# Block products of the triangular inverse in four 32-row array tiles instead of two 64-row tiles

## The chip, the cores and the metric

The kernel runs on one core of a Trainium2 chip. The metric is the device time of one execution in microseconds (us). Before the change the median of three runs is 4128.65 us (4125.22 to 4132.72). TensorE is the matmul engine, VectorE (DVE), ScalarE (ACT) and GpSimd (POOL) the others; SyncE (SP) issues some of the DMAs.

## The reference

Two blocks of two layers each, batch 1, 512 tokens, width 1024, all in float32. The first block is a hybrid of retention and HGRN2 with a gated MLP; the second has sliding-window attention, an RWKV-7 recurrence, a gated MLP and an embedding layer. Only the recurrence of the second block matters here:

```
def rwkv7_scan(r, w, k, v, a, b):           # 16 heads of 64 channels, 512 tokens
    def step(state, inp):
        r_t, w_t, k_t, v_t, a_t, b_t = inp
        sa = jnp.einsum('bhvk,bhk->bhv', state, a_t)
        state = (state * w_t[:, :, None, :] + sa[..., None] * b_t[:, :, None, :]
                 + v_t[..., None] * k_t[:, :, None, :])
        return state, jnp.einsum('bhvk,bhk->bhv', state, r_t)
    ...
```

## The kernel before

The stage is the function `rwkv_b`, run once in each of the two layers of the second block. It works on 8 pairs of heads (`PAIRS`). The 128 partitions hold two heads of 64 channels; the 512 columns are 8 chunks (`NC`) of 64 tokens (`C`). Inside a chunk the recurrence is a triangular system: with A the strictly lower 64x64 matrix of the decayed products of a and b, the kernel needs the inverse of (I - A) for each head and each chunk. The chunks themselves then follow each other in a chain.

The inverse is built by doubling. It starts from 1x1 and 2x2 diagonal blocks and runs over five levels, `INV_LEVELS = (2, 4, 8, 16, 32)`. At the level with number n, two neighbouring diagonal blocks of size n become one of size 2n. Three block products make a level, each a call of `products`:

- `lower` (the order's rows with bank 3): the matrix `mabt` (a buffer of `gate`) by the inverse so far, `xx` (a buffer of `rw_z`). ScalarE copies bank 3 to `pp` (also in `gate`) at L2116, a helper's line for nearly all of its operations in this stage.
- `inverse` (bank 5): the inverse so far by `pp`. VectorE merges the result into `xx` with a mask, by a predicated copy at L2378.
- `inverse_t` (bank 4): the transposed result, merged into `xt` (`rw_xt`) at the same line.

The last level has no `inverse`, since only the transposed form is used afterwards. A call of `products` issues one 64x64 matmul for each chunk and each head, 16 in all; a head's matmul uses the rows and columns of its own half of the array, so the two heads sit in two array tiles. Only the last matmul of a call signals. The mask takes from the result only the blocks that the level joins.

TensorE's order is written out by hand: in pair p, between every two products, `chain_on` issues one of the 24 steps of the chunk chain of pair p-1 (L1933 to L1949, also 64x64 matmuls). After each step VectorE makes a small copy (L2276, L2278, L2281) that the next step waits for. Pair 0 has no such steps between its products. The head of a pair (`dense`) holds the projections (L228 to L230, 128x512) of the pair's inputs, with weights that are streamed from HBM through a ring by GpSimd's queue.

All engines' instruction streams are unrolled over layers and pairs, so each matmul is an instruction of its own in the program.

Of the kernel before, what the change touches and what calls it, by code (L numbers as in the profile page):

```python
# [1438 lines left out]
C = 64  # L1439
NC = S // C  # L1440
# [367 lines left out]
def rwkv_b(run, io, l, ws, again, nxt, y_all, y_hi, y_lo, gate):  # L1808

    with ExitStack() as ctx:  # L1810
        sc = Stage(run, ctx, f"rw{l}")
        half = run.eps[:, 3:4]
        banks, par = run.banks, run.par_b[:, l, :]
# [3 lines left out]
        v, mabt, pp = ks, lw, cum  # L1817
        e0, e1, kn, yq = run.w[:, 0, :], run.w[:, 1, :], run.w[:, 2, :], run.acc
        z = sc.sb("z", [P, 2, S + 1])
        xx = [z[:, i, 1:S + 1] for i in range(2)]  # L1820
# [6 lines left out]
        at_, rt, mak, mrb, mrk, xt, bt, ktt, vt = ([e[:, :], o[:, :]] for e, o in zip(even, odd))  # L1827
# [17 lines left out]
        cx_made, cx_kept, xcx_made, xcxt_made = (sc.sem("cx_made"), sc.sem("cx_kept"), sc.sem("xcx_made"),  # L1845
                                                 sc.sem("xcxt_made"))
# [6 lines left out]
        LEVELS_ = len(INV_LEVELS)  # L1853
# [16 lines left out]
        def read(name, p):  # L1870

            i = place[name, p]
            who = order[i][3]
            return who, sum(e[3] is who for e in order[:i + 1])
# [6 lines left out]
        def cut(c):  # L1881
            return slice(c * C, (c + 1) * C)
# [25 lines left out]
        def _(pe):  # L1908
            def claim(name, p):

                i = place[name, p]
                for e in reversed(order[:i]):
                    if e[2] == order[i][2]:
                        pe.wait_ge(*read(*e[:2]))
                        break
                return bank(name, p)[:, :]

            def whole(name, p, lhs, rhs_, signal):
                pe.matmul(claim(name, p), lhs, rhs_, start=True, stop=True).then_inc(signal, 1)  # L1919
# [32 lines left out]
            def products(out, lhs, rhs_, signal):  # L1952

                for c in range(NC):
                    for s_ in heads:
                        mm = pe.matmul(banks[out][s_, cut(c)], lhs[s_, cut(c)], rhs_[s_, cut(c)], start=True, stop=True)  # L1956
                mm.then_inc(signal, 1)

            def dense(p):
                def decays():  # L1960
                    if p == 0:
                        pe.wait_ge(wa_made, 1)
                    pe.wait_ge(low_in[p % 2], 32 * (p // 2 + 1))
                    if p:
                        pe.wait_ge(f_free, 3 * p)
                        pe.wait_ge(x_made, 5 * p)
                    whole("w", p, lr[0:64, p % 2, :], wa[0:64, :], lr_made)
                    whole("a", p, lr[64:128, p % 2, :], wa[64:128, :], lr_made)

                if p:  # L1970
                    decays()
                if p >= 2:
                    pe.wait_ge(ysq_made, p - 1)
                    pe.wait_ge(xt_made, 6 * p)
                    whole("var", p - 2, bones[:, :], yq[:, :], var_made)
                ws.project(pe, claim("k", p), hh, hl)
                if p == 0:
                    decays()
                ws.project(pe, claim("r", p), hh, hl)
                pe.wait_ge(sq_made, p + 1)  # L1980
                if p:
                    pe.wait_ge(cx_kept, 5 * p)
                whole("ssq", p, bones[:, :], e0, ssq_made)
                ws.project(pe, claim("v", p), hh, hl)
                if p == 0:
                    pe.wait_ge(gd_made, 2)
                out = claim("g", p)
                pe.matmul(out, g2[:, p % 2, 0, :], gd[:, 0, :], start=True, stop=False)
                pe.matmul(out, g2[:, p % 2, 1, :], gd[:, 1, :], start=False, stop=True).then_inc(g_made, 1)
                pe.wait_ge(rk_made, p + 1)  # L1990
                whole("bonus", p, bones[:, :], kp, bon_made)
# [33 lines left out]
            def lower(p, i):  # L2025
                n = LEVELS_ * p + i
                pe.wait_ge(x_made, n + 1)
                if i:
                    pe.wait_ge(cx_kept, n)
                else:  # L2030
                    pe.wait_ge(f_free, 3 * p + 2)
                products(3, mabt, xx[p % 2], cx_made)

            def inverse(p, i):
                n = LEVELS_ * p + i
                pe.wait_ge(cx_kept, n + 1)
                pe.wait_ge(xt_made, 6 * p + i + 1)
                if i == 0:
                    pe.wait_ge(*read("bonus", p))
                products(5, xt[p % 2], pp, xcx_made)  # L2040

            def inverse_t(p, i):
                pe.wait_ge(cx_kept, LEVELS_ * p + i + 1)
                pe.wait_ge(xt_made, 6 * p + i + 1)
                if i == 0 and p >= 2:
                    pe.wait_ge(*read("var", p - 2))
                products(4, pp, xt[p % 2], xcxt_made)

            again.wait(pe, "lo", KD)
            for n in range(3):  # L2050
# [3 lines left out]
            for p in range(PAIRS):  # L2054
                steps = iter(range(24))

                def chain_on():
                    if p:
                        chain(p - 1, next(steps))
                dense(p)  # L2060
                chain_on()
                for j in range(2):
                    scores(p, j)
                    chain_on()
                turned(p, 0)
                chain_on()
                for j in range(2, 5):
                    scores(p, j)
                    chain_on()
                for i in range(LEVELS_):  # L2070
                    lower(p, i)
                    chain_on()
                    if i < 2:
                        turned(p, i + 1)
                        chain_on()
                    if i < LEVELS_ - 1:
                        inverse(p, i)
                    chain_on()
                    inverse_t(p, i)
                    chain_on()  # L2080
# [1027 lines left out]
```

## Time and profile before

| | |
|---|---|
| median of the runs | 4128.65 us |
| profiled execution | 4121.49 us |
| its span, first to last instruction | 4119.7 us |
| TensorE busy | 3838.9 us, 93% |
| TensorE weight loads busy | 3113.2 us, 76% |
| VectorE busy | 2031.1 us, 49% |
| ScalarE busy | 1740.7 us, 42% |
| GpSimd busy | 792.4 us, 19% |
| DMA | 628.97 MB, mean 153 GB/s |
| mean granted clock | 0.979 of full speed |

How to read it: "PE" is TensorE's matmuls, "PEld" its weight loads, which overlap them. Matmuls are pipelined and the ends of their records are modelled, so a busy PE is not an array at its peak. A row names the line of the kernel, the engine, the operation, what is written and what is read. A releaser is what ended an idle time; "issue" is an idle time that ended with no semaphore that the profile shows.

### The profile page before, as it was taken

The page shows a single profiled execution, that of the slowest core. Times are in us where ns is not written, and L with a number is a line of the kernel's source. Part 1 is how long each engine was busy: PE and PEld are TensorE (multiplying, and loading weights), DVE is VectorE, ACT ScalarE, POOL GpSimd, SP SyncE. Part 2 cuts the span into 40 slices and gives each one's busy share as a digit, 9 for nine tenths or more (in the row PEclk, how much of TensorE's full clock was granted, in tenths as well). Part 3 has the DMA queues.
Part 4 walks back from the last instruction along what each step waited for, and adds up shares of the span by engine and source line. Part 5 has one row for each costly group of instructions (what it writes and reads, how often), then busy time and mean ns, then how long its engine had stood idle before and what let it go on. Part 6 is the DMA issues. An engine that isn't in the chain of part 4 may idle for free.

```text
span 4119.7 us, 69619 instructions
## 1 busy us (share of the span) xinstructions
PE 3838.9 (93%) x28892; PEld 3113.2 (76%) x28892; DVE 2031.1 (49%) x3591; ACT 1740.7 (42%) x2560; POOL 792.4 (19%) x1108
## 2 busy tenths in 40 slices
PE   5888999999899999999999999998999999989997
PEld 4676778777678876877787778876777888778885
DVE  5575663126633226445564376324635556356603
ACT  3364322336543236555553332234745554342223
POOL 1111222221122221210001222222120000222221
PEclk9999999999999999999999999999999999999998
DMA  8954999875388885652223879986473222678995
GB/s 281 248 115 106 264 295 194 201 174 127 83 172 193 191 176 133 147 133 54 64 55 89 183 161 193 192 177 148 106 177 79 63 57 59 146 155 195 193 193 134
DMA packets 190026, 628.97 MB, mean 153 GB/s; under 512 B 22800, under 2 KB 28176, under 8 KB 189328
## 3 DMA queue, kind: packets, MB, share of 16 engines
q0 software_dynamic: 158976, 549.52, 60.6%
q1 hardware_dynamic: 28176, 70.79, 4.9%
q8 instruction: 230, 3.77, 0.4%
q10 hardware_dynamic: 2560, 4.20, 0.3%
q14 instruction: 84, 0.69, 0.1%
HBM read 612.89 MB, written 2.10 MB: 149 GB/s over the span
## 4 chain that ended last, share of the span: by engine, by line
PE 48%; ACT 5%; DVE 5%; DMA 2%; issue 1%; SPq 0%; ACTq 0%; DVEq 0%; POOL 0%
PE bank L228 11%; PE bank L230 11%; PE bank L229 11%; PE bank L1956 5%; ACT gate L2116 1%; PE bank L1642 1%; PE bank L1919 1%; PE bank L1945 1%; ACT L2116 1%; PE bank L1624 1%; DVE rw_z L2378 1%; PE bank L1615 1%; DMA at_sw<-at_raw 1%; ACT acc L2116 1%; PE bank L1933 0%
## 5 line engine op out<-in xcount | busy, mean ns | idle before, releaser
L228 PE MATMUL bank<-h_hi,w_hi 128*128 128x512 f32 x2608 | 1067.1, 409 | 47.9 <-DMA w_lo<-in_b_wup 10.4
L229 PE MATMUL bank<-h_lo,w_hi 128*128 128x512 f32 x2608 | 1024.9, 393 | 0.0
L230 PE MATMUL bank<-h_hi,w_lo 128*128 128x512 f32 x2608 | 1024.9, 393 | 0.0
L161 ACT ACTIVATE w_lo<-w_hi 128x1024 fp32r<-128x1024 f32 (+2 forms) x552 | 555.8, 1011 | 985.9 <-DMA w_hi<-in_a_wgv 301.7
L228 PEld LDWEIGHTS bank<-h_hi,w_hi 128*128 128x128 f32 x2608 | 495.2, 190 | 182.4 <-issue 55.2
L229 PEld LDWEIGHTS bank<-h_lo,w_hi 128*128 128x128 f32 x2608 | 495.3, 190 | 105.7 <-issue 10.5
L230 PEld LDWEIGHTS bank<-h_hi,w_lo 128*128 128x128 f32 x2608 | 494.4, 190 | 106.7
L2116 ACT ACTIVATE gate<-bank 128x512 f32<-128x512 f32 x96 | 57.3, 597 | 267.0 <-PE bank L1956 266.8
L228 PE MATMUL bank<-fa_y_hi,w_hi 128*128 128x512 f32 x352 | 137.1, 390 | 0.0
L230 PE MATMUL bank<-fa_y_hi,w_lo 128*128 128x512 f32 x352 | 137.1, 389 | 0.0
L229 PE MATMUL bank<-fa_y_lo,w_hi 128*128 128x512 f32 x352 | 137.1, 389 | 0.0
L229 PE MATMUL bank<-fb_y_lo,w_hi 128*128 128x512 f32 x352 | 137.1, 389 | 0.0
L228 PE MATMUL bank<-fb_y_hi,w_hi 128*128 128x512 f32 x352 | 137.1, 389 | 0.0
L230 PE MATMUL bank<-fb_y_hi,w_lo 128*128 128x512 f32 x352 | 137.0, 389 | 0.0
L2647 DVE SCALAR_TENSOR_TENSOR fb_work<-fb_work,par_b 128x512 f32<-128x512 f32 x176 | 132.3, 752 | 6.3
L1388 DVE TENSOR_SCALAR fa_conv<-fa_a_in,par_a 128x512 f32<-128x512 f32 x44 | 21.5, 490 | 226.7 <-ACT fa_a_in L1334 226.1
L2644 DVE TENSOR_TENSOR fb_work<-bank,rstd 128x512 f32<-128x512 f32 x88 | 60.9, 692 | 122.8 <-PE bank L230 122.4
L128 POOL DMA_DIRECT2D w_hi<-in_b_wrkv x48 | 31.4, 655 | 458.2 <-PE bank L230 458.2
L132 POOL DMA_DIRECT2D w_lo<-in_a_wgv x96 | 90.2, 946 | 137.0 <-ACT w_lo L161 129.4
L2657 DVE COPY fb_work<-bank 128x512 f32<-128x512 f32 x16 | 11.1, 691 | 210.2 <-ACT w L319 210.2
L1421 DVE SCALAR_TENSOR_TENSOR x<-bank,mods,x 128x512 f32<-128x512 f32 x16 | 12.0, 751 | 204.1 <-PE bank L230 204.1
L319 ACT ACTIVATE w<-x 128x512 f32<-128x512 f32 x72 | 45.5, 632 | 151.0 <-DVE x L1421 72.0
(458 smaller groups left out, 7602.3 us busy)
## 6 DMA issues: line engine op xcount, KB each, us to landing
w_hi<-in_a_wgv POOLq DMA_DIRECT2D x80, 512.0 KB, 5.5
w_lo<-in_a_wgv POOLq DMA_DIRECT2D x80, 512.0 KB, 7.8
w_hi<-in_b_wup POOLq DMA_DIRECT2D x80, 512.0 KB, 5.1
w_lo<-in_b_wup POOLq DMA_DIRECT2D x80, 512.0 KB, 7.3
w_hi<-in_a_wh POOLq DMA_DIRECT2D x48, 512.0 KB, 4.6
w_lo<-in_a_wh POOLq DMA_DIRECT2D x48, 512.0 KB, 5.3
fa_ada_raw<-in_ada SPq DMA_DIRECT2D x48, 512.0 KB, 8.2
w_hi<-in_b_wrkv POOLq DMA_DIRECT2D x48, 512.0 KB, 4.5
```

The source lines that it names most:

```text
L132: pool.dma_start(self.lo[:, self.span(n)], self.pieces[n][0], accum_op=ALU.add)\
L161: st.do(st.eng.activation(self.lo[:, s], self.hi[:, s].bitcast(F32), ACT.Copy, scale=-1.0), (self.neg_made, n + 1))
L228: pe.matmul(out, self.hi[:, a], hh[:, k0 + k, :], start=first and k == 0, stop=False)
L229: pe.matmul(out, self.hi[:, a], hl[:, k0 + k, :], start=False, stop=False)
L230: mm = pe.matmul(out, self.lo[:, a], hh[:, k0 + k, :], start=False, stop=last and k == ks - 1)
L319: st.do(st.eng.activation(self.run.w[:, k % 2, :], src, ACT.Square), self.sig("sq", 8 * part + k + 1))
L1615: mm = pe.matmul(banks[2 + g][:, 256 * j:256 * (j + 1)], rot[rows, p % 2, ib * P:(ib + 1) * P], kpad[rows, kb, ib * P:(ib + 2) * P], start ...
L1624: mm = pe.transpose(banks[4 + i // 4][:, (i % 4) * P:(i % 4 + 1) * P], s[:, u % 3, i * P:(i + 1) * P], run.eye[:, :])
L1956: mm = pe.matmul(banks[out][s_, cut(c)], lhs[s_, cut(c)], rhs_[s_, cut(c)], start=True, stop=True)
L2116: st.do(act.activation(*args, **how), signal)
L2644: do(dve.tensor_tensor(a_in[:, b, 2:S + 2], banks[n % 4][:, :], run.rstd[:, :], ALU.mult), (a_free, n + 1))
L2647: do(dve.scalar_tensor_tensor(out=conv[:, b, :], in0=a_in[:, b, j:j + S], scalar=col(f"conv{j}", n), in1=conv[:, b, :], op0=ALU.mult, op1= ...
```

## The change

A second helper, `small_products`, cuts each chunk's 64x64 product into its four 32x32 quarters on the partitions: for each quarter q of the 128 partitions it multiplies the diagonal block of 32 rows and 32 columns. `block_products(i)` takes it for the first four levels (block sizes 2, 4, 8 and 16, whose joined blocks are at most 32x32) and the old helper for the last. The two off-diagonal quarters of a chunk are no longer computed at those levels; the masks of these levels don't read them. A call issues 32 matmuls of 32x32 where it had 16 of 64x64. There are 12 such calls in a pair, 192 in the two layers.

```diff
+            def small_products(out, lhs, rhs_, signal):
+
+                for c in range(NC):
+                    for q in range(4):
+                        q_, t = slice(q * C // 2, (q + 1) * C // 2), slice(c * C + q % 2 * C // 2, c * C + (q % 2 + 1) * C // 2)
+                        mm = pe.matmul(banks[out][q_, t], lhs[q_, t], rhs_[q_, t], start=True, stop=True)
+                mm.then_inc(signal, 1)
+
+            def block_products(i):
+                return small_products if i < LEVELS_ - 1 else products
+
...
-                products(3, mabt, xx[p % 2], cx_made)
+                block_products(i)(3, mabt, xx[p % 2], cx_made)
...
-                products(5, xt[p % 2], pp, xcx_made)
+                block_products(i)(5, xt[p % 2], pp, xcx_made)
...
-                products(4, pp, xt[p % 2], xcxt_made)
+                block_products(i)(4, pp, xt[p % 2], xcxt_made)
```

The program's order on TensorE, before the change, in pair 1 of the first of the two layers, from the product into bank 5 at the third level to the product into bank 3 at the fourth. L1941 to L1949 are chain steps of pair 0; `rw0_z` is `xx`, `rw0_xt1` is `xt`, `gate0` holds `mabt` and `pp`.

```order
L1956 MATMUL bank5<-gate0,rw0_xt1 64x64 x16
L1941 MATMUL bank6<-rw0_rhs,rw0_xt0 64x64 x2
L1956 MATMUL bank4<-rw0_xt1,gate0 64x64 x16
L1945 MATMUL bank7<-rw0_mrb0,rw0_uu 64x64 x2
L1948 MATMUL bank6<-rw0_uu,rw0_bt0 64x64
L1949 MATMUL bank6<-rw0_vt0,rw0_ktt0 64x64
L1948 MATMUL bank6<-rw0_uu,rw0_bt0 64x64
L1949 MATMUL bank6<-rw0_vt0,rw0_ktt0 64x64
L1956 MATMUL bank3<-rw0_z,gate0 64x64 x16
```

And the same place after the change:

```order
L1964 MATMUL bank5<-gate0,rw0_xt1 32x32 x32
L1941 MATMUL bank6<-rw0_rhs,rw0_xt0 64x64 x2
L1964 MATMUL bank4<-rw0_xt1,gate0 32x32 x32
L1945 MATMUL bank7<-rw0_mrb0,rw0_uu 64x64 x2
L1948 MATMUL bank6<-rw0_uu,rw0_bt0 64x64
L1949 MATMUL bank6<-rw0_vt0,rw0_ktt0 64x64
L1948 MATMUL bank6<-rw0_uu,rw0_bt0 64x64
L1949 MATMUL bank6<-rw0_vt0,rw0_ktt0 64x64
L1964 MATMUL bank3<-rw0_z,gate0 32x32 x32
```

The products keep their places, banks and waits, and each has 32 matmuls where it had 16; the chain steps between them are the same 64x64 matmuls.

In pair 0, before the change, the first two levels stand without chain steps (L2022 is a transpose):

```order
L1956 MATMUL bank3<-rw0_z,gate0 64x64 x16
L2022 MATMUL bank1<-eye,w 128x128 x4
L1956 MATMUL bank5<-gate0,rw0_xt0 64x64 x16
L1956 MATMUL bank4<-rw0_xt0,gate0 64x64 x16
L1956 MATMUL bank3<-rw0_z,gate0 64x64 x16
L2022 MATMUL bank0<-eye,w 128x128 x4
L1956 MATMUL bank5<-gate0,rw0_xt0 64x64 x16
L1956 MATMUL bank4<-rw0_xt0,gate0 64x64 x16
L1956 MATMUL bank3<-rw0_z,gate0 64x64 x16
```

And after it:

```order
L1964 MATMUL bank3<-rw0_z,gate0 32x32 x32
L2033 MATMUL bank1<-eye,w 128x128 x4
L1964 MATMUL bank5<-gate0,rw0_xt0 32x32 x32
L1964 MATMUL bank4<-rw0_xt0,gate0 32x32 x32
L1964 MATMUL bank3<-rw0_z,gate0 32x32 x32
L2033 MATMUL bank0<-eye,w 128x128 x4
L1964 MATMUL bank5<-gate0,rw0_xt0 32x32 x32
L1964 MATMUL bank4<-rw0_xt0,gate0 32x32 x32
L1964 MATMUL bank3<-rw0_z,gate0 32x32 x32
```

Here the small products follow each other directly, but for the transposes. On the other engines the order is unchanged.

## Rows read from the trace of the kernel before

**Rows 1.** The page: engine busy time and records; the chain that ended last, by line.

```profile
PE 3838.9 (93%) x28892; PEld 3113.2 (76%) x28892; DVE 2031.1 (49%) x3591; ACT 1740.7 (42%) x2560; POOL 792.4 (19%) x1108
...
PE bank L228 11%; PE bank L230 11%; PE bank L229 11%; PE bank L1956 5%; ACT gate L2116 1%; PE bank L1642 1%; PE bank L1919 1%; PE bank L1945 1%; ACT L2116 1%; PE bank L1624 1%; DVE rw_z L2378 1%; PE bank L1615 1%; DMA at_sw<-at_raw 1%; ACT acc L2116 1%; PE bank L1933 0%
```

**Rows 2.** Windows: one pair; engine busy us (records), clock, DMA share, GB/s.

```profile
1946.10:2001.10 55.00, 52.48 (x958) 43.83 (x958) 33.37 (x64) 29.31 (x46) 4.48 (x7) 1.00 0.27 64
```

**Rows 3.** Groups by line and form: product records; busy us, mean ns, idle before.

```profile
L1956 PE MATMUL bank<-rw_z,gate 64*64 64x64 f32 x2560 | 92.2, 218 | 2.0 <-issue 2.0
```

**Rows 4.** Timeline, one level: start us, us, engine, operation, count, idle before.

```profile
1974.42 1.15 PE L1956 MATMUL bank<-rw_z,gate 64*64 64x64 f32 x32
...
1975.60 0.60 ACT L2116 ACTIVATE gate<-bank 128x512 f32<-128x512 f32 x1 [2.70 <-PE bank L1956]
...
1976.25 1.15 PE L1956 MATMUL bank<-gate,rw_xt 64*64 64x64 f32 x32 [0.22 <-ACT gate L2116]
...
1977.51 0.73 DVE L2378 COPY_PREDICATED rw_z<-rw_im,bank 128x512 f32<-128x512 int32 x1 [1.39 <-PE bank L1956]
1978.28 0.23 DVE L2278 COPY rw_uu<-bank 128x64 f32<-128x64 f32 x1
...
1978.56 0.33 PE L1945 MATMUL bank<-rw_mrb,rw_uu 64*64 64x64 f32 x4
...
1978.96 1.15 PE L1956 MATMUL bank<-rw_z,gate 64*64 64x64 f32 x32
```

**Rows 5.** Windows of 10 ns at the start of a product, records of L1956 alone.

```profile
1976.25:1976.26 0.01, 0.01 (x2) 0.01 (x2) 1.00 0.00 0
```

**Rows 6.** Timeline: from 64x64 chain matmuls to 128x128 transposes.

```profile
1970.34 0.33 PE L1949 MATMUL bank<-rw_vt,rw_ktt 64*64 64x64 f32 x4
...
1970.61 0.66 PE L2022 MATMUL bank<-eye,w 128*128 128x128 f32 x4
```

**Rows 7.** The page: TensorE's instruction queue, packets, MB, share of 16 engines.

```profile
q8 instruction: 230, 3.77, 0.4%
```

**Rows 8.** Window 1964:1984: TensorE records; DMA, GB/s in 40 slices, and its queue.

```profile
1964.00:1984.00 20.00, 19.11 (x564) 1.00 0.01 3
...
GB/s 0 0 0 0 0 0 0 33 0 0 0 0 0 0 0 0 0 33 0 0 0 0 0 0 0 0 33 0 0 0 0 0 0 0 0 0 33 0 0 0
...
q8 instruction: 4, 0.07, 1.3%
```

**Rows 9.** Chain of waits in three windows: start us, us, what.

```profile
1804.00 1.84 PE bank L1956 x55
1805.84 1.09 issue
...
2019.79 0.89 issue
...
3095.26 1.04 issue
```

**Rows 10.** DMA: 1804.4:1804.6, 1809.5:1809.7, 2018.3:2018.45, 2021.8:2022.0, 2130.4:2130.7, 2133.8:2134.0.

```profile
q8 instruction: 1, 0.02, 30.2%
...
q8 instruction: 1, 0.02, 37.8%
...
q8 instruction: 1, 0.02, 39.5%
...
q8 instruction: 1, 0.02, 39.8%
...
q8 instruction: 1, 0.02, 19.3%
...
q8 instruction: 1, 0.02, 35.2%
```

**Rows 11.** Chain of waits, one level of pair 0: start us, us, what.

```profile
1811.99 3.24 PE bank L1956 x96
...
1815.25 0.61 ACT gate L2116
```

## The prediction

> **What bounds the kernel now.** I read the page first: TensorE is busy for 93% of the span, and the chain of work that ended last lies almost wholly on its lines; L1956, the line of the block products, has 5% of it [rows 1]. The table by windows shows one whole pair of the recurrence: 55.0 us, 52.48 of them with TensorE busy, at a granted clock of 1.00 [rows 2]. So what TensorE spends or saves here moves the end, unless something it waits for takes the time. The changed operations are x2560 records of 64x64 in a group like the one in [rows 3]. A float32 matmul of the source stands in the trace as two matmul and two weight-load records, so a product of 16 matmuls is the "x32" of the timeline.
>
> The timeline of one level of a pair shows what its 4.54 us (1974.42 to 1978.96) are made of [rows 4]. The product into bank 3 takes 0.93 us of TensorE (1.15 less the 0.22 of its last record [rows 3]); ScalarE copies it for 0.60; the product into bank 5 starts at 1976.25 after 0.22 us of idle; VectorE merges it from 1977.51 on (0.73), then copies rw_uu at 1978.28; TensorE takes up the chain step at 1978.56. The product into bank 4 lies beside this. Two of the three products are thus on a loop TensorE, ScalarE, TensorE, VectorE, and the third fills what would be idle.
>
> **Part one, the products get shorter.** A product after the change has 32 source matmuls, so 64 records, each on half the rows with half the columns. What does one cost? Within 10 ns two records of the present product start, in two tiles (x2) [rows 5]; in the steady state 32 of them start in 0.93 us, so one tile takes a new record every 58 ns. A 128-column record is started every (0.66 - 0.275) / 3 = 0.11 us, if its last record lasts about 0.275 [rows 6]: the interval goes with the columns. For 32 columns I estimate 31 ns per tile, and 16 records in each of four tiles that run side by side: 16 x 31 = 0.50 us, 0.43 less per product. Upper bound, if four tiles don't overlap better than two: 64 x 29 ns = 1.87 us. Lower bound: nothing in the rows speaks for less than 0.43. I take 0.50, since the rows show tiles that start within nanoseconds of one another.
>
> **Part two, changes of array shape.** In pairs 1 to 7 every small product stands between chain steps of 64x64 (the order piece of pair 1). The last record of L1949 starts at about 1970.34 + 0.33 - 0.22 = 1970.45, and the first record of the 128x128 shape behind it at 1970.61 [rows 6]: 0.16 us, where the same shape would follow after 0.03. No row shows 64x64 followed by 32x32. Between 0 and about 0.13 us for each of 24 new changes in a pair; I take 0.12, near the row's. Those ahead of a product into bank 5 or of the chain step at 1978.56 hide in waits that are there today; the one ahead of the product into bank 3 does not.
> The Trainium skill ("TensorEngine Tiling (Array Packing)", Key Properties) says that changing the tiling mode drains TensorE and changing only the tile does not; the trace agrees for 64 to 128, and no row shows 64 to 32. Left out, the sum below stays, since part three hides this cost.
>
> **Part three, twice the instructions.** This is what decides. TensorE's instructions come by a queue of their own, q8: 230 transfers, 3.77 MB, 16 KB each [rows 7]. There are 28892 matmul records [rows 1], so one transfer brings what 28892 / 230 = 126 of them need, with as many weight loads. The quiet window 1964 to 1984 holds 564 matmul records and four such transfers, the only traffic, 4.5 to 5 us apart [rows 8].
> Does TensorE ever wait for one? The chain of waits has three gaps called "issue" in the middle of a product, where no semaphore is awaited: 1.09 us up to 1806.94, 0.89 us up to 2020.67, 1.04 us up to 3096.30 [rows 9]. For the first two I looked where q8 had started [rows 10]: at 1804.4 to 1804.6 and at 2018.3 to 2018.45, 2.3 to 2.5 us before the work went on. The next transfers start at 1809.5 to 1809.7 and 2021.8 to 2022.0. I read this as two buffers: the next block is asked for when the sequencer enters the one before, and if its work runs out first, TensorE stands. A full turn (resume, next transfer, resume) took 1.2 + 2.3 = 3.5 us in one case and 2.7 + 2.4 = 5.1 in the other, under weight traffic; the closest two transfers that I found are 2130.4:2130.7 and 2133.8:2134.0, 3.3 us apart [rows 10]. So one block, 126 matmul records, costs at least about 3.3 us however short the matmuls are. Today's pace is 20 us / (564 / 126) = 4.47 us a block: just above. I take 3.45 us for a turn without much traffic.
>
> The sum for a pair of 1 to 7: the window's 564 records become 564 + 12 x 32 = 948, or 7.55 blocks. Their own work would take about 17.7 us (part one and two), but the blocks come every 3.45 us: 26.0 us. A block is in hand at the start, worth 4.47 - 3.45 = 1.0. So 25.0 instead of 20.0: **5.0 us more**, 14 times over two layers, 70 us. The waits of the loop and the changes of shape lie inside the new stalls.
> Pair 0 has no chain steps. A level takes 3.90 us today, 1811.99 to 1815.90, 96 records [rows 11]; with 192 records, 1.53 blocks, 5.27 us: 1.37 more, four levels, less 1.0: 4.5 us, twice: 9. Together **79 us**. Work behind the stretch starts later by as much, since TensorE has hardly any idle time to give back [rows 2]. The copies and masks of ScalarE and VectorE keep their shapes and cost nothing more. The profiled execution took 4121.5 us; 4121.5 + 79 = 4200.5. The median of the runs, 4128.65, stands 7.2 above it: 4207.
> With a turn of 3.1 us (the transfer starts sooner in quiet stretches) the same sum gives 2 us a pair and 34 in all, 4163; with 3.9, 9 us a pair and 141 in all, 4270.
>
> **The rivals.** *Faster: the supply doesn't bind.* If more blocks were ahead than I think, the level's loop would lose 0.43 twice and gain one change of shape: 4.54 - 0.86 + 0.12 = 3.80. With the levels 0 and 1, which hold transposes too, I get 2.3 to 3 us per pair, and in pair 0 up to 1.3 us a level: 14 x 2.6 + 10 = 46 us less, 4083. The three gaps speak against it. It decides if a block's turn is under (20.0 - 2.6) / 7.55 = 2.3 us.
> The Trainium skill ("Runtime: NRT & Kernel Launch", Instruction fetch mechanics) gives TensorE a buffer of 2048 instructions, refilled in blocks of 256, with the fetch mostly hidden: by that rule it would be this rival. The block size fits the trace; the gaps, each some 2.3 us behind a late transfer, don't fit so deep a buffer.
> *The turn is short.* At 3.0 us or a bit less the loss is 10 to 30 us, at 2.5 it is nothing: between 4121 and 4160.
> *The clock falls.* TensorE would stand about a third of the time in the stretch. Its clock stayed 1.00 through today's pauses [rows 2, 11]. Should it fall to 1.2 GHz, the small products take about 0.97 us, which the stalls mostly hide, but the projections behind run at half speed for a few us: 2 to 3 us a pair, 40 more, 4250.
> *The four tiles don't overlap.* 1.87 us for a product: then two products last 3.74 us, more than a turn, and the level grows by 0.93 twice plus what the third no longer finds idle, about 2.5 us: 14 x 10 + 22 = 162, 4290.
>
> **How the numbers follow.** Forecast (turn of 3.34 to 3.9 us) 0.70; short turn 0.09; faster 0.08; clock 0.09; no overlap 0.04. I leave the faster case and the last out and range from 4160 to 4268. A measurement can tell about 0.2% (8 us) from no change: the short turn gives 0.03 to "same", the rest of it is slower. So faster 0.08, same 0.03, slower 0.89.
>
> **What would show it.** Right: the changed products have 64 records; most of their groups are broken by "issue" gaps of about 1 us that wait for nothing; q8 has some 279 transfers (230 + 192 x 32 / 126), in the stretch 3.3 to 3.6 us apart; a pair takes about 60 us instead of 55. An unbroken product of 0.50 us shows part one right. Wrong: q8 transfers closer than 3 us, or a pair under 55 us. A granted clock of 0.5 in a pair would show the clock rival, an unbroken product of 1.9 us the last.

## The result and the profile after

The changed kernel takes 4274.51 us (median of 4 runs, 4265.05 to 4283.13), the kernel before on the same chip 4130.03. The ratio is 1.0354, 95% interval 1.0342 to 1.0367: slower by 144 us. The forecast was slower by 79 us, 4207, with a range up to 4268. The direction and the mechanism of the supply were right, the size wasn't, and the time lies just outside the range.

The page of the profiled execution after (span, busy time, clock in 40 slices, TensorE's instruction queue, chain by engine):

```profile
span 4270.8 us, 81907 instructions
PE 3905.0 (91%) x35036; PEld 3151.1 (74%) x35036; DVE 2030.6 (48%) x3591; ACT 1741.5 (41%) x2560; POOL 791.9 (19%) x1108
...
PEclk9999999999999999988989999999988889999998
...
q8 instruction: 278, 4.55, 0.4%
...
PE 48%; ACT 5%; DVE 4%; issue 3%; DMA 2%; SPq 0%; ACTq 0%; DVEq 0%; POOL 0%
```

Against [rows 1, 7]: 6144 matmul records more, 48 more transfers on q8 (278 instead of 230), and TensorE busy for 66 us more, while the span of the profiled executions grew by 151. The rest is waiting: the chain of waits has 3% of the span as "issue", where it was 1% before. A second thing is new: the clock falls to 8 tenths in slices of the recurrence.

The changed products, by line and form, over both recurrences (records, busy us, mean ns, idle ahead of them and what ended it):

```profile
L1964 PE MATMUL bank<-rw_xt,gate 32*32 32x32 f32 x4096 | 66.4, 217 | 30.4 <-issue 30.4
L1964 PE MATMUL bank<-gate,rw_xt 32*32 32x32 f32 x4096 | 64.7, 219 | 19.6 <-issue 16.0 <-ACT gate L2127 2.8 <-DVE rw_bonus L2423 0.4
L1964 PE MATMUL bank<-rw_z,gate 32*32 32x32 f32 x4096 | 63.0, 210 | 35.0 <-issue 34.7
```

In [rows 3] such a group had 2.0 us of "issue" ahead of it. Here the three have 81 (30.4 + 16.0 + 34.7), for which no semaphore was awaited; more lies ahead of the chain steps between them.

One typical pair by stage: head and scores, the four lower levels, the last level up to the next pair (engine busy us with records, granted clock, DMA share, GB/s). First the kernel before, then the one after:

```profile
2056.83:2074.80 17.97, 17.90 (x281) 14.34 (x282) 13.78 (x25) 11.79 (x18) 2.44 (x4) 1.00 0.63 150
2074.80:2094.19 19.39, 18.50 (x543) 17.14 (x540) 10.85 (x25) 5.41 (x12) 0.00 (x0) 1.00 0.01 3
2094.19:2111.48 17.29, 16.11 (x149) 12.34 (x145) 8.74 (x16) 12.10 (x17) 1.80 (x3) 1.00 0.18 42
```

```profile
3343.04:3361.15 18.11, 18.11 (x280) 14.49 (x280) 13.62 (x24) 11.79 (x18) 2.47 (x4) 1.00 0.69 152
3361.15:3387.77 26.62, 19.89 (x923) 16.94 (x922) 11.26 (x25) 5.41 (x12) 0.00 (x0) 0.85 0.02 5
3387.77:3406.08 18.31, 17.19 (x147) 13.43 (x144) 8.42 (x16) 12.10 (x17) 1.80 (x3) 0.93 0.20 37
```

The pair went from 54.65 to 63.04 us: 0.14 in the first stage, 7.23 in the levels, 1.02 behind them, where the kernel is unchanged but the clock is 0.93. In pair 0 of the second layer the levels went from 15.64 to 24.50 and what is behind them from 14.99 to 18.17:

```profile
3096.57:3112.21 15.64, 13.99 (x400) 12.70 (x395) 7.24 (x10) 6.36 (x15) 0.48 (x1) 1.00 0.30 70
3112.21:3127.20 14.99, 14.30 (x118) 11.45 (x117) 6.70 (x9) 8.45 (x12) 1.44 (x2) 1.00 0.25 57
```

```profile
3170.23:3194.73 24.50, 14.43 (x779) 12.45 (x778) 7.18 (x10) 5.41 (x12) 0.00 (x0) 0.53 0.17 41
3194.73:3212.90 18.17, 17.47 (x121) 13.64 (x118) 6.69 (x9) 8.45 (x12) 1.44 (x2) 0.79 0.20 44
```

That is 12 us. All sixteen pairs, read in the same way from the two traces, give the account of the profiled executions: the levels of the fourteen pairs 1 to 7 took 19.5 us in the mean before and 26.9 after (from 24.8 to 29.2), 103 us more together; the rest of these pairs took 19 us more; pair 0 took 10.4 us more in the first layer and 12.2 in the second. Together these are 145 us. The other 6 of the 151 lie almost wholly ahead of the first product, where nothing was changed: the profiled execution before was one of the faster ones.

The timeline of the levels of the typical pair after, rows of the products alone (start us, us from the first start to the last end, idle ahead):

```profile
3361.15 0.70 PE L1964 MATMUL bank<-rw_z,gate 32*32 32x32 f32 x59
...
3362.89 0.25 PE L1964 MATMUL bank<-rw_z,gate 32*32 32x32 f32 x5 [1.03 <-issue]
...
3364.46 0.75 PE L1964 MATMUL bank<-gate,rw_xt 32*32 32x32 f32 x64
...
3375.38 1.07 PE L1964 MATMUL bank<-rw_z,gate 32*32 32x32 f32 x64
...
3385.55 0.37 PE L1964 MATMUL bank<-gate,rw_xt 32*32 32x32 f32 x19 [1.79 <-issue]
```

An unbroken product (3364.46) takes 0.75 less its last record of 0.19, so 0.56 us, where [rows 4] and the prediction have 0.93. So the product itself did get shorter. Others are broken, 59 records and then, 1.03 us later, the last 5. The one at 3375.38 is unbroken but slow: the clock is at 1.2 GHz there.

```profile
3361.15:3373.00 11.85, 9.06 (x443) 7.52 (x440) 6.08 (x14) 4.21 (x10) 0.00 (x0) 1.00 0.02 5
3373.50:3379.50 6.00, 5.47 (x208) 4.81 (x212) 1.82 (x4) 0.60 (x1) 0.00 (x0) 0.50 0.02 5
```

Transfers in the window 3358 to 3388, 40 slices of 0.75 us (seven of q8's eight are the 22s; weights move only up to 3361):

```profile
GB/s 98 180 197 126 0 11 0 0 22 0 0 0 0 22 0 0 0 0 22 0 0 0 0 22 0 0 0 0 22 0 0 0 0 22 0 0 0 0 22 0
...
q8 instruction: 8, 0.13, 1.9%
```

Every fifth slice holds one: six intervals in 22.5 us, about 3.75 each, in a stretch whose work is very uneven. In the levels of all fourteen pairs there are 86 such intervals, from 3.30 to 4.48 us, 3.77 in the mean.

### The profile page after: what moved, and what is told of

Read it like the earlier page. It is cut to its first block, busy times and chain, and to the rows that moved or that the text cites. A ratio compares the mean times of both kernels' runs of the same rounds, so it can differ in the third digit from the quotient of the medians.

```text
span 4270.8 us, 81907 instructions
## 1 busy us (share of the span) xinstructions
PE 3905.0 (91%) x35036; PEld 3151.1 (74%) x35036; DVE 2030.6 (48%) x3591; ACT 1741.5 (41%) x2560; POOL 791.9 (19%) x1108
## 4 chain that ended last, share of the span: by engine, by line
PE 48%; ACT 5%; DVE 4%; issue 3%; DMA 2%; SPq 0%; ACTq 0%; DVEq 0%; POOL 0%
PE bank L228 11%; PE bank L229 10%; PE bank L230 10%; PE bank L1964 4%; PE bank L1956 2%; PE bank L1642 1%; PE bank L1919 1%; PE bank L1945 1%; ACT L2127 1%; PE bank L1933 1%; PE bank L1624 1%; ACT gate L2127 1%; PE bank L1615 1%; PE bank L1941 1%; DMA at_sw<-at_raw 1%
## 5 line engine op out<-in xcount | busy, mean ns | idle before, releaser
L132 POOL DMA_DIRECT2D w_lo<-in_b_wup x96 | 86.4, 907 | 120.5 <-ACT w_lo L161 113.0
```

The source lines that it names most:

```text
L132: pool.dma_start(self.lo[:, self.span(n)], self.pieces[n][0], accum_op=ALU.add)\
```

## The experiments

The theory (**supply**): TensorE gets its instructions in blocks that 126 matmul records use up, and a block costs a turn of some 3.3 to 3.8 us, whatever the matmuls take. The rivals: the new changes between array shapes cost the time (**shapes**); 32x32 matmuls in four tiles are slow in themselves (**tiles**); and of the size, the granted **clock** has a share. A first version, which left out every second chunk and so had the old number of instructions, gave no time; e5 below takes its place. The times and ratios are against the kernel before on the same chip.

| kernel | median us | ratio to before, 95% interval |
|---|---|---|
| changed kernel | 4274.51 | 1.0354 (1.0342 to 1.0367) |
| e6_bf16_twice | 4274.51 | 1.0364 (1.0347 to 1.0381) |
| e5_bf16_once | 4116.67 | 0.9981 (0.9971 to 0.9990) |
| e10_bf16_64 | 4068.23 | 0.9856 (0.9838 to 0.9874) |
| e12_bf16_mixed | 4070.06 | 0.9854 (0.9833 to 0.9875) |
| e8_fill | 4257.93 | 1.0323 (1.0308 to 1.0339) |
| e9_stream | 4266.46 | 1.0345 (1.0327 to 1.0363) |
| e7_two_levels | 4189.03 | 1.0161 (1.0144 to 1.0178) |
| e4_lower_only | 4135.83 | 1.0024 (1.0014 to 1.0033) |
| e11_few | 4121.66 | 0.9989 (0.9976 to 1.0001) |
| e2_pad | 4293.38 | 1.0408 (1.0383 to 1.0434) |
| e3_pad_projections | 4231.39 | 1.0254 (1.0232 to 1.0277) |

### The number of instructions alone

A bfloat16 matmul of the source is one matmul and one weight load where float32 is two and two: a group of products has 2048 matmul records in e5 and 4096 in the changed kernel. So the same small products can be had with half the instructions, and, issued twice, with the old number again.

```diff
-                        mm = pe.matmul(banks[out][q_, t], lhs[q_, t], rhs_[q_, t], start=True, stop=True)
+                        mm = pe.matmul(banks[out][q_, t], *([x[q_, t].bitcast(mybir.dt.bfloat16)[:, 1::2] for x in (lhs, rhs_)]),
+                                       start=True, stop=True)
```

Once:

> The changed kernel, but the 32 source matmuls of a small product read only the upper halves of the float32 words, as bfloat16 (less exact; the lower halves are left out). Such a matmul is one matmul and one weight load instead of two and two: 64 instructions in a product, as many as in the kernel before, with the same four tiles and the same 24 changes of shape in a pair. Theory supply: 4.47 blocks of 3.77 us, less 1 in hand, so the stretch of levels takes about 16 us instead of 19.4 (before) and 26.8 (changed): 4050 to 4100 us, faster than both. Rival shapes (the changes between 64x64 and 32x32 cost the time): about 4275, as the changed kernel. Rival tiles (32x32 matmuls are slow in themselves): about half of the loss, 4200.

Twice, in a loop of two around that matmul:

> The kernel of the run with bfloat16 halves, but each of the small matmuls is issued twice, the second over the first: 128 instructions in a product, as in the changed kernel. Shapes and tiles as there, and the result as in the run with one. Theory supply: only the number of instructions matters, so the time of the changed kernel, 4255 to 4295, and 180 to 230 us more than the run with one. Rival shapes: no difference between once and twice. Rival own time of the matmuls: at most 0.25 us more in each of 192 products on the loop: 50 us more than once.

Measured: 4116.67 once, 4274.51 twice, 158 us more (180 to 230 were expected; the rival of the matmuls' own time allowed 50). Against the kernel before on its own chip twice is 149.5 us slower, the changed kernel 144.5; that the two medians agree to the hundredth is chance. The matmuls are of another type: their groups are busy for 50 us where those of the changed kernel are busy for 65. The three groups of e6, then one pair of it in the levels:

```profile
L1965 PE MATMUL bank<-rw_xt,gate 32*32 32x32 bf16 x4096 | 50.8, 184 | 36.1 <-issue 36.1
...
L1965 PE MATMUL bank<-rw_z,gate 32*32 32x32 bf16 x4096 | 50.5, 182 | 39.3 <-issue 38.2 <-DVE rw_z L2391 1.0
...
L1965 PE MATMUL bank<-gate,rw_xt 32*32 32x32 bf16 x4096 | 49.2, 184 | 24.3 <-issue 20.8 <-ACT gate L2129 3.0 <-DVE rw_bonus L2425 0.5
```

```profile
1938.86:1965.13 26.27, 20.36 (x923) 17.19 (x922) 10.80 (x25) 5.41 (x12) 0.00 (x0) 0.62 0.02 4
```

A part of what the matmuls saved reappears as "issue" (95 us instead of 81), and the levels take 26.27 us as against 26.62 (in the mean of fourteen pairs 26.5 against 26.9). In the levels the number of instructions sets the time; the work behind them hardly does. The run with one has all 24 changes of shape too, so the shapes rival, which wanted 4275 for it, falls, and so does tiles, which wanted 4200.

The once run is faster than before by 8 us only, where 25 to 75 were expected. Its pair, levels and what follows:

```profile
2131.18:2147.73 16.55, 13.95 (x540) 11.18 (x538) 10.75 (x25) 5.41 (x12) 0.00 (x0) 0.83 0.03 5
2147.73:2166.84 19.11, 18.03 (x148) 14.29 (x145) 8.41 (x16) 12.11 (x17) 1.83 (x3) 0.88 0.17 38
```

The levels came to 16.55 us, as expected (about 16), 2.8 less than before. But 1.8 of it are lost again behind them, where float32 products of 64x64 run at the low clock: 1.71 us for one in the chain of waits, 0.93 at full clock.

```profile
1983.37 1.71 PE bank L1956 x32
```

The typical pair also flatters this run: in four of the fourteen the clock is at 0.67 or less and the levels take 18.3 to 18.9 us; the mean is 17.3. So here, unlike in the changed kernel, the long levels are those with the lowest clock.

### Work in the place of the waits

```diff
+                pe.matmul(banks[out][:, 0:2 * P], run.eye[:, :], run.eye[:, :].unsqueeze(1).broadcast_to([P, 2, P]), start=True, stop=True)
                 for c in range(NC):
                     for q in range(4):
```

> The changed kernel, with one long matmul (128x128 weights, 256 moving columns, 4 instructions) ahead of each small product, into the place that the product then overwrites: 0.44 us of work for TensorE with hardly any instruction. Theory supply: the long matmuls lie in the waits for instructions, the stretch stays at 26 to 28 us. What the clock costs: if the pauses make it fall, it stays at 1.00 here, and the last level and what follows go back from 18.5 to 17.3 us in a pair: 4240 to 4275. Rival (TensorE isn't waiting for instructions, but is busy or waits for its partners): 12 x 0.44 us more in a pair, 4350 or above.

Measured: 4257.93, though TensorE got more to do. That is 16.6 us faster than e6 on the same chip; against the changed kernel, each compared with the kernel before on its own chip, it is 11.6 us (132.9 slower instead of 144.5). One filler, one product behind it, and the group of the fillers:

```profile
3355.50 0.70 PE L1961 MATMUL bank<-eye 128*128 128x256 f32 x2
3356.13 0.75 PE L1965 MATMUL bank<-rw_z,gate 32*32 32x32 f32 x64
```

```profile
L1961 PE MATMUL bank<-eye 128*128 128x256 f32 x384 | 138.3, 443 | 8.5 <-ACT gate L2128 3.8 <-issue 3.5
```

A filler took 0.63 us (3356.13 less 3355.50), 192 of them 121 us. Most of that doesn't show in the time: it went into the waits, and "issue" fell to 9.2% of the chain in the levels of one pair, where the changed kernel has 24.7%. The first stage, the levels and what is behind them:

```profile
3330.04:3349.62 19.58, 18.77 (x282) 14.82 (x283) 14.30 (x25) 11.78 (x18) 2.46 (x4) 1.00 0.61 138
3349.62:3376.25 26.63, 24.18 (x943) 18.13 (x943) 10.59 (x25) 5.41 (x12) 0.00 (x0) 1.00 0.02 4
3376.25:3393.59 17.34, 16.15 (x146) 12.38 (x146) 8.40 (x15) 12.12 (x17) 1.80 (x3) 1.00 0.20 42
```

From the first small product on, the levels take 26.63 us, as without the fillers (26.62; in the mean of fourteen pairs 26.7 against 26.9), at a clock of 1.00 instead of 0.85: in the changed kernel's levels the low clock costs nothing that can be seen, since the supply is later. Behind them it is 17.34 instead of 18.31. One filler in twelve is not hidden: that of the first product stands ahead of the levels, in the first stage, which takes 19.58 instead of 18.11 us. So the pair as a whole is no shorter (63.55 against 63.04), and the gain of the run is what the clock gave back, less some 10 us of fillers in the open (16 x 0.63). The clock's share, read behind the levels: of the 19 us that the rest of the fourteen pairs lost, 7 are still there in e8 when the fillers in the open are taken off, so 12 go to the clock, and 6 in the two pairs 0. That makes about 18 us of 144, an estimate from the two traces.

### The turn by itself

```diff
+                if p == 3 and i == 0:
+                    for k in range(630):
+                        for q in range(4):
+                            q_, t = slice(32 * q, 32 * q + 32), slice(k % 16 * 32, k % 16 * 32 + 32)
+                            pe.matmul(banks[3][q_, t], *([x[q_, t].bitcast(mybir.dt.bfloat16)[:, 1::2] for x in (mabt, xx[1])]),
+                                      start=True, stop=True)
                 products(3, mabt, xx[p % 2], cx_made)
```

> The kernel before, with a stream of 2520 tiny matmuls (32x32, bfloat16, four tiles, one matmul and one weight load each: 20 blocks of 126) at one place of each layer, ahead of the first product of the levels of pair 3; the product then overwrites what they wrote. It measures the disputed turn by itself, with no semaphore and no weight traffic in it. The run with such matmuls once showed 32 of them in 0.39 us, so 126 need 1.55 us of TensorE. Theory supply: the transfers of instructions are one turn apart all the same. If the turn is what the changed kernel showed (3.77 us), 75 us for each stream, 4275; if it is the 3.45 of the prediction, 69 us, 4263; at 3.3, 4257. If the supply doesn't bind: 31 us each, 4187.

Measured: 139.7 us more for the two streams, 70 for each stream of 20 blocks. By the sum in the expectation that is 3.49 us a block, nearer to 3.45 than to 3.77. But the interval of the ratio is 7 us wide to either side, 3.7 for a stream, and the sum left out the block in hand, so the time alone can't tell the two values apart. The trace can. Its chain of waits shows the turn bare (start us, us, what):

```profile
3332.16 1.22 PE bank L2036 x116
3333.38 2.25 issue
3335.63 1.22 PE bank L2036 x123
3336.85 2.25 issue
3339.10 1.22 PE bank L2036 x122
3340.32 2.80 issue
3343.12 1.22 PE bank L2036 x115
```

About 120 of the 126 records in 1.22 us, then 2.25 us of nothing, over and over. From resume to resume it is 3.47 us, and once 4.02 (3339.10 to 3343.12). The transfers beside it, in the window 3331 to 3341 with slices of 0.25 us:

```profile
GB/s 0 0 0 0 0 0 0 0 0 66 0 0 0 0 0 0 0 0 0 0 0 0 0 66 0 0 0 0 0 0 0 0 0 0 0 0 0 66 0 0
```

They start in the slices at 3333.25, 3336.75 and 3340.25: 1.1 to 1.4 us after TensorE resumes (3332.16, 3335.63, 3339.10), and 2.1 to 2.4 us before it resumes again (2.6 to 2.9 in the turn of 4.02). This is the turn as the prediction read it from two gaps. The transfers of the other stream, in a window of 80 us with slices of 2 us, each 8 one transfer:

```profile
GB/s 141 0 8 0 8 0 8 0 8 0 8 0 8 0 8 8 0 8 0 8 0 8 0 8 0 8 8 0 8 0 8 0 8 0 8 0 8 8 0 0
...
q8 instruction: 21, 0.34, 1.8%
```

Twenty of the 21 stand from the slice at 1964 to the one at 2034: 19 turns in 70 us, 3.7 on average, though many are 3.47. Twenty of these, less the block in hand at the start, are the 70 us by which the time grew; in the trace the levels that hold the streams are 75 and 72 us longer.

```profile
3326.00:3342.00 16.00, 5.27 (x561) 4.77 (x550) 0.00 (x0) 0.00 (x0) 0.00 (x0) 0.51 0.02 5
```

TensorE's clock was 0.51 there, and the turn is as long as where the clock was 1.00: in the changed kernel the transfers keep their 3.75 us through the stretch at 1.00 and the one at 0.50 shown above. No dependence on that clock is seen.

### Doses

Only the product into bank 3 small:

```diff
-                block_products(i)(5, xt[p % 2], pp, xcx_made)
+                products(5, xt[p % 2], pp, xcx_made)
-                block_products(i)(4, pp, xt[p % 2], xcxt_made)
+                products(4, pp, xt[p % 2], xcxt_made)
```

> Only the product into bank 3 (first of each level) is made of 32x32 blocks, in all four lower levels; the two others stay 64x64. A third of the added instructions. Theory supply: 692 records or 5.5 blocks in the window of a pair, at 3.7 us a turn 20.3 less 1 in hand, against 20.0 before and about 18.5 of own work: the loss and the gain cancel, 4115 to 4150. Rivals shapes and tiles: a third of the loss, about 4178. If the supply did not bind: 0.43 less in each level, 4100 or below.

Only levels 0 and 1 small:

```diff
-                return small_products if i < LEVELS_ - 1 else products
+                return small_products if i < 2 else products
```

> Only levels 0 and 1 are made of 32x32 blocks, levels 2 and 3 stay 64x64: half of the added instructions. Theory supply with a block in hand at the start: 6 times 32 records more are 1.52 blocks or 5.7 us of fetching, less the slack of about 0.7 us in each block of the first two levels and the 1.3 us in hand: 2.5 to 3 us in a pair, 4165 to 4190. A theory in which each changed product costs the same expects half of the loss, 4202.

Measured: 8.1 and 64.0 us more than before. A third of the instructions costs 6% of the loss, half of them 44%. Neither is proportional: there is a slack to be used up first, as the theory says. Shapes and tiles wanted 4178 for e4 and the same cost for each product in e7 wanted 4202. That the same number would hurt less when spread over four levels fits, but no run shows it. The levels of a pair (e4, then e7):

```profile
2079.77:2099.59 19.82, 17.89 (x668) 16.23 (x666) 10.69 (x25) 5.42 (x12) 0.00 (x0) 1.00 0.02 4
```

```profile
3478.15:3501.16 23.01, 19.60 (x732) 17.56 (x730) 10.68 (x25) 5.41 (x12) 0.00 (x0) 0.93 0.02 4
```

In e7 it is 3.6 us instead of the 2.5 to 3 expected (3.9 in the mean of fourteen pairs). That sum used a turn of 3.75, so the turn isn't what it had wrong: the slack or the block in hand was taken as too large. Which of the two stays open.

A dose that fits into the slack was meant to gain:

```diff
-                block_products(i)(3, mabt, xx[p % 2], cx_made)
+                (small_products if p and i in (0, 2) else products)(3, mabt, xx[p % 2], cx_made)
```

> A version meant to gain: only the product into bank 3 of levels 0 and 2, in pairs 1 to 7, is made of 32x32 blocks, 28 products in all instead of 192, full float32. Theory supply: 64 records more in a pair are 0.51 blocks, 1.9 us of fetching, against the 1.3 us in hand and the slack of 0.7 us in each of the 4.5 blocks: it fits in, and each such product gives back up to 0.43 us: 0.3 to 0.8 us in a pair, 5 to 11 us less than before, 4115 to 4122. If there is less slack than the mean pace says: within 5 us of before. Rivals shapes and tiles: 28/192 of the loss, 20 us more.

The levels of a typical pair take 19.01 us instead of 19.39 (window 1858.10 to 1877.11), but over the fourteen pairs they take 272.5 us together instead of 273.5, far from the 0.3 to 0.8 expected in each. The runs give 5 us less, and the interval of the ratio holds 1: no gain is shown. What the run does show is that these 28 products don't cost the 20 us that the rivals shapes and tiles wanted.

### Without the limit: what shape and tiles are worth

Products of 64x64 in two tiles that read bfloat16 halves as in e5, half the instructions of the kernel before (e10):

> The kernel before, but in the four lower levels the 16 source matmuls of 64x64 in two tiles read the upper halves as bfloat16 (less exact): 32 instructions in a product, half of the kernel before, and no new change of shape. Beside the run with 32x32 blocks in bfloat16 once (64 instructions, 0.39 us a product, 24 changes of shape), which took 4117. With neither short of instructions, this shows what four tiles are worth without that limit. A product is about 0.47 us. Theory supply: not short, the stretch of levels is set by ScalarE's and VectorE's work at 16 to 17 us in a pair, and the time is within 15 us of that run: 4100 to 4130, more than that only if the clock falls more. If the changes of shape cost time there, this one is up to 14 x 2 us faster: below 4095.

And the same with the product into bank 3 of 32x32 blocks, bfloat16 too (e12):

> The kernel with 64x64 products of bfloat16 halves (4068), but the product into bank 3 of the four lower levels is made of 32x32 blocks, in bfloat16 too: 8 new changes of shape in a pair, and instructions in a window of 564 - 8 x 16 = 436 records, 3.5 blocks or 13 us of fetching beside 15.1 us of work, so the supply is not short. It measures the changes of shape and the four tiles without it. 32 records of 32x32 took 0.39 us, 16 of 64x64 took 0.29. If a change costs nothing on the path: 4 x 0.1 us in a pair more, 4075. If a change costs 0.12 to 0.16 us (the estimate of the prediction) on the path: 8 of them are 1.0 to 1.3 us in a pair, 4085 to 4095. If the changes are what made the run with 32x32 in all three products slower by 2.9 us in a pair, a third of that or more: 4085 to 4090 as well, and in the levels rather than in the last level.

Measured: 4068.23 and 4070.06. The levels and what is behind them in e10, then the levels in e12:

```profile
2116.64:2131.76 15.12, 11.47 (x351) 9.91 (x349) 10.84 (x25) 5.41 (x12) 0.00 (x0) 1.00 0.01 4
2131.76:2149.05 17.29, 16.11 (x149) 12.34 (x145) 8.71 (x16) 12.11 (x17) 1.79 (x3) 1.00 0.18 41
```

```profile
1960.19:1975.27 15.08, 11.46 (x412) 9.73 (x411) 10.68 (x25) 5.42 (x12) 0.00 (x0) 1.00 0.01 3
```

For e10 I had expected 4100 to 4130, and the run missed that by over 30 us: the levels are at 15.1, not 16 to 17. The clock stayed at 1.00 in the levels of thirteen of the fourteen pairs 1 to 7 (0.81 in the other), though not in pair 0, where it fell as in the changed kernel:

```profile
1811.29:1823.73 12.44, 7.78 (x207) 6.32 (x203) 7.20 (x11) 6.81 (x16) 0.88 (x1) 0.64 0.48 108
```

Two things differ in e5, whose levels took 16.55: it has 540 records there, 4.3 blocks, and its clock is 0.83. No run tells them apart. Eight changes of shape a pair, in e12, cost nothing that can be seen (15.08 against 15.12); the chain waits for VectorE there, and they lie inside. Where nothing covers it, at the end of the first stage, it shows once in a pair: 18.11 us in the changed kernel, 17.97 in the one before; and likewise 18.10, 18.07 and 18.09 in e4, e7 and e12, which change shape at that place, against 17.97 in e10, which doesn't.

### A padding that said little

Tiny matmuls, 33 columns of weights and one moving column in the shape of 64x64, one ahead of each matmul of the kernel before in the four lower levels (e2), or as many ahead of the projections (e3):

```diff
+                        pe.matmul(banks[out][s_, c * C:c * C + 1][0:33, :], lhs[s_, c * C:c * C + 33], rhs_[s_, c * C:c * C + 1],
+                                  start=True, stop=True)
                         mm = pe.matmul(banks[out][s_, cut(c)], lhs[s_, cut(c)], rhs_[s_, cut(c)], start=True, stop=True)
```

```diff
+            def tiny(out):
+                for c in range(24):
+                    for s_ in heads:
+                        pe.matmul(out[s_, 8 * c:8 * c + 1][0:33, :], run.eye[s_, 0:33], run.eye[s_, 0:1], start=True, stop=True)
+                return out
...
-                ws.project(pe, claim("k", p), hh, hl)
+                ws.project(pe, tiny(claim("k", p)), hh, hl)
```

> The kernel before with its products of 64x64 in two tiles; in the four lower levels each of the 16 source matmuls has a tiny one ahead of it (33 columns of weights, 1 moving column, same array shape, into the place that the real one then overwrites). So the number of instructions in each place is that of the changed kernel, and neither the shape nor the number of tiles changes. Theory supply: the time of the changed kernel, 4240 to 4290, with the stretch of levels at 26 to 27 us in a pair. Rivals shapes and tiles: the kernel before plus the own time of the tiny matmuls, at most 0.3 us in a product: 4130 to 4180. If the granted clock stays at 1.00 here, the difference to the changed kernel is what the clock costs.

> The kernel before with the same tiny matmuls, as many in each pair (192), but in four groups of 48 ahead of the projections, where matmuls of 512 columns use instructions slowly. Theory supply: the blocks come in time, and only the own time of the tiny matmuls shows, 15 to 20 ns each: 3 to 4 us in a pair, 4150 to 4195, clearly below the run with the same matmuls in the levels. Rival own time (the tiny matmuls or any added instruction cost the same wherever they stand): the same time as that run, about 4250 or more.

Measured: 4293.38 and 4231.39. The first looks like the supply theory, but its levels say otherwise:

```profile
2122.72:2150.04 27.32, 26.44 (x928) 25.47 (x926) 10.48 (x25) 5.41 (x12) 0.00 (x0) 1.00 0.02 4
```

TensorE is busy for 26.44 of 27.32 us: it isn't waiting. A tiny matmul costs about 34 ns (e3: a pair of 61.11 instead of 54.65 us, 6.5 for 192 of them), twice what I had taken, so 192 of them alone fill the levels to about the time that the supply would want. The two can't be told apart in e2, and it is no evidence for either; besides, the clock fell in the levels of three of its sixteen pairs, which took 34 to 40 us. e3 shows that instructions in front of long matmuls bring no waiting: TensorE is busy for 59.64 us of that pair instead of 52.51, and idle for less than before (1.5 instead of 2.1). Its time lies above the 4150 to 4195 expected, by the price of a tiny matmul.

## Why the prediction was off

**Part one, the product: right.** 0.50 us was forecast, 0.56 measured, four tiles side by side.

**Part two, changes of shape: right that they hide.** Measured 0.14 us where nothing covers one (0.12 was taken), and nothing for the eight that e12 has in the levels. The Trainium skill ("TensorEngine Tiling (Array Packing)", Key Properties) says that a change of mode drains TensorE; those 0.14 us agree.

**Part three, the supply: the mechanism right, the turn mis-sized.** This is the step that failed. The prediction's sum took 3.45 us for a turn; the 86 intervals between transfers in the levels are 3.77 in the mean. By the prediction's own rule (7.33 blocks, less 4.47 - 3.77 = 0.70 in hand) that gives 26.9 us, which is the measured mean of the levels. The value was chosen from one turn of 3.5, which was put together from the parts of two gaps, and from the closest pair of transfers, 3.3. But the closest of many is the low end of a spread, here from 3.30 to 4.48. The sum needs the mean. Levels of 7.4 us more instead of 5.0 are 33 us in fourteen pairs. With 3.9, the upper bound that the prediction worked out, a pair loses 9 us, more than it did; that this sum, 4270, still stays under the measured time is due to the next two terms.

**Pair 0: too little by some 14 us.** The prediction gave it 4.5 us in a layer; measured are 10.4 and 12.2. In the second layer its levels took 8.9 more, and 3.2 more went behind them at a clock of 0.79. With a turn of 3.77 four levels of 1.53 blocks, less the block in hand, take 22.4 us instead of the forecast's 20.1; measured are 24.50. The rest lies at the start: two transfers are 6.6 us apart there (3167.3 and 3173.9), and the chain of waits has its longest stall behind them:

```profile
3172.82 3.38 issue
```

The five turns after it are 3.5 to 3.7. In those 6.6 us TensorE also waits for VectorE, and weights move (a DMA share of 0.17 over the levels, in a later pair 0.02); which of the two made the transfer late no run shows.

**The clock: a term that the forecast had at nothing.** The prediction gave the clock rival 0.09, as an alternative with a time of its own. It happened beside the forecast rather than in its place, since it came with the forecast's own stalls. The clock falls to 1.2 GHz for a part of every pair but costs nothing that can be seen in the levels, and behind them about 1 us in a pair, not 2 to 3: some 18 us in all with the two pairs 0. (The prediction names rows 11 for today's clock of 1.00; they show no clock, but the row of pair 0 before, above, does.)

**The sum of the shortfall.** Of the 65 us by which the forecast fell short, 33 are the turn in fourteen pairs, 19 the rest of these pairs (12 by the clock, 2 by the change of shape at the end of the first stage, the others not separated), and 14 pair 0 (6 by the clock). These are read from single profiled executions, and the runs of one kernel differ by several us.

**The other rivals didn't happen.** The closest two transfers of q8 are 3.30 us apart, not under 3; four tiles do overlap; and the supply does bind. The Trainium skill ("Runtime: NRT & Kernel Launch", Instruction fetch mechanics) has the fetch mostly hidden. This case's runs differ: in e9 2.25 of every 3.47 us are spent waiting for it.

**What would show it, checked.** 278 transfers (279 forecast); broken groups with "issue" gaps of about 1 us, up to 1.8 in the typical pair and 3.4 in pair 0; a pair of 63 us, not 60; transfers 3.77 us apart in the mean, not 3.3 to 3.6; and, as the sign of the clock rival, a granted clock of 0.50.

## What to carry to other kernels

Count instructions, not only cycles. In this kernel a stretch that gives TensorE less than about 3.8 us of work for every 126 matmul records (30 ns a record) takes its time from the number of records. There, splitting a matmul into smaller ones makes it slower however well the tiles overlap. Fewer instructions are the way out: the 64x64 products in bfloat16 (e10) took 58 us less than the kernel before, at lower precision, though they also halve TensorE's work, and no run separates the two. The place to look is the chain of waits: "issue" gaps in the middle of a group, with the transfers of the instruction queue a constant distance apart. When a bound is read from the closest of a few events, use it for the lower end and look for the mean to put into the sum; and put the price of what a stall may bring with it, as the clock here, into the forecast's range and not beside it.

## What the runs showed of the hardware

- In the levels of the changed kernel a turn of the instruction queue took 3.77 us in the mean (3.30 to 4.48) for 126 matmul records with their weight loads, in the streams of e9 mostly 3.47 and about 3.7 in the mean. In e9 it is 2.1 to 2.9 us from the start of a transfer to the resume, and 1.1 to 1.4 us from there to the next transfer. It was as long at a clock of 0.5 as at 1.00.
- A matmul of 32x32 in bfloat16, four tiles side by side, was started every 10 ns as long as there were instructions (122 in 1.22 us in e9, at a granted clock of 0.51).
- The granted clock fell to 0.50 in the changed kernel, in e5, in e6 and in e9, and stayed at 1.00 in the levels of thirteen of the fourteen pairs 1 to 7 of e10 and of e12, although TensorE was idle for as large a share of them there (3.65 of 15.12 us against 6.73 of 26.62); in their pairs 0 it fell too. So the idle share alone doesn't explain it, and what does stays open. With long matmuls in the waits (e8) it stayed at 1.00 in the levels of thirteen of the sixteen pairs, and behind all of them.
- Work added to TensorE made the kernel faster: with 121 us of fillers it took 16.6 us less than e6 on the same chip, and 11.6 less than the changed kernel when each is compared with the kernel before.
